# Expert weights dealt to partitions in 16 KB runs, gather and transposes on strided columns

## What is computed

```
n2 = rms_norm(h, norm2_w)
top_v, top_i = top_k(n2 @ w_router + b_router, 4);  gates = softmax(top_v)
for each expert e, for its tokens xb:
    gu   = xb @ w_gu[e] + b_gu[e]            # w_gu   (32, 1024, 2048)
    gate = min(gu[:, :1024], 7);  up = clip(gu[:, 1024:], -7, 7)
    act  = gate * sigmoid(1.702 * gate) * (up + 1)
    y    = act @ w_down[e] + b_down[e]       # w_down (32, 1024, 1024)
    h   += y * gate_of_the_token
```

## Time and profile before

| | |
|---|---|
| time, three runs | 1054.03, 1056.91, 1062.96 us (median 1056.91) |
| span of the profiled execution | 1053.6 us |
| what lies around the span, against the median | 3.3 us |
| PE busy | 1002.0 us (95%) |
| DVE, ACT, POOL busy | 212.1, 147.8, 17.8 us |
| moved by DMA | 417.84 MB, mean 397 GB/s |
| DMA packets | 80940, of which 48688 under 8 KB |

### The profile page before, as it was taken

One profiled execution on the slowest core, in us unless ns is written; L12 is line 12 of the kernel. 1 busy time (PEld: TensorE's weight loads), 2 busy tenths in 40 slices (PEclk: granted clock), 3 DMA queues, 4 the chain that ended last, 5 costly groups with the idle time before them and its releaser, 6 DMA issues.

```text
span 1053.6 us, 12628 instructions
## 1 busy us (share of the span) xinstructions
PE 1002.0 (95%) x5069; PEld 436.9 (41%) x5069; DVE 212.1 (20%) x620; ACT 147.8 (14%) x273; POOL 17.8 (2%) x12
## 2 busy tenths in 40 slices
PE   6989999999999999999999999999999999999997
PEld 4455444444444444433443333334433444434443
DVE  1765311111111111111111111111111111101112
ACT  0332111111110111111111011111110111101111
POOL 0050000000000000000000000000000000000000
PEclk9989999999999999999999999999999999999999
DMA  9995899999999999999999999999999999999994
GB/s 328 276 385 205 304 416 415 416 417 416 419 418 418 417 417 418 418 416 419 419 418 417 417 417 417 418 419 420 418 418 417 409 409 417 417 416 417 418 418 192
DMA packets 80940, 417.84 MB, mean 397 GB/s; under 512 B 8336, under 2 KB 9104, under 8 KB 48688
## 3 DMA queue, kind: packets, MB, share of 16 engines
q1 hardware_dynamic: 75840, 415.91, 97.8%
q10 hardware_dynamic: 5072, 1.51, 0.8%
HBM read 416.35 MB, written 1.05 MB: 396 GB/s over the span
## 4 chain that ended last, share of the span: by engine, by line
PE 54%; SPq 20%; DMA 16%; DVE 5%; ACTq 2%; issue 1%; ACT 1%
PE ps L986 26%; SPq L310 20%; DMA ring<-w_gu_dram 16%; PE ps L1053 13%; PE ps L950 7%; PE ps L964 3%; PE ps L857 2%; DVE PT L763 1%; ACTq L424 1%; ACTq L419 1%; PE ps L1029 1%; ACT PR L462 1%; PE ps L1070 0%; PE ps L837 0%; DVE PR L611 0%
## 5 line engine op out<-in xcount | busy, mean ns | idle before, releaser
L986 PE MATMUL ps<-ring,PT 128*64 128x512 f32 x2008 | 453.7, 595 | 17.1 <-DMA ring<-w_gu_dram 15.5
L986 PEld LDWEIGHTS ps<-ring,PT 128*64 128x64 f32 x2008 | 140.2, 137 | 309.7 <-issue 270.0
L1053 PE MATMUL ps<-ring,PT 128*64 128x512 f32 x1020 | 225.9, 595 | 3.4
L751 DVE TENSOR_SCALAR tT<-ps 128x256 f32<-128x256 f32 x64 | 27.2, 425 | 702.1 <-PE ps L986 702.1
L950 PEld LDWEIGHTS ps<-qk,N 128*128 128x128 f32 x1056 | 120.4, 192 | 21.3 <-issue 21.3
L1053 PEld LDWEIGHTS ps<-ring,PT 128*64 128x64 f32 x1020 | 70.5, 137 | 138.7 <-issue 127.9
L950 PE MATMUL ps<-qk,N 128*128 128x64 f32 x1056 | 124.9, 276 | 0.4 <-DVE qk L724 0.4
L510 ACT ACTIVATE tT<-tT 128x256 f32<-128x256 f32 x64 | 26.7, 418 | 484.4 <-DVE tT L751 484.4
L964 PE MATMUL ps<-PT 64*128 64x512 f32 x256 | 63.6, 615 | 0.8 <-ACT PT L516 0.8
L516 ACT COPY PT<-ps 128x512 f32<-128x512 f32 x32 | 18.8, 587 | 218.7 <-PE ps L1053 218.7
L510 ACT ACT_TABLE_LOAD x32 | 41.1, 1283 | 0.6
(11 more groups left out here) (158 smaller groups left out, 328.2 us busy)
## 6 DMA issues: line engine op xcount, KB each, us to landing
ring<-w_gu_dram SPq DMA_DIRECT2D x121, 2048.0 KB, 25.5
ring<-w_down_dram SPq DMA_DIRECT2D x61, 2048.0 KB, 30.5
ring<-w_gu_dram SPq DMA_DIRECT2D x9, 1024.0 KB, 26.0
ring<-w_down_dram SPq DMA_DIRECT2D x8, 512.0 KB, 21.6
ring<-w_in_dram SPq DMA_DIRECT2D x8, 384.0 KB, 7.3
ring<-w_in_dram SPq DMA_DIRECT2D x2, 1024.0 KB, 13.0
ring<-w_out_dram SPq DMA_DIRECT2D x1, 2048.0 KB, 19.2
ring<-w_out_dram SPq DMA_DIRECT2D x2, 1024.0 KB, 24.1
```

Of the source, the lines that this page charges most:

```text
L751: nc.vector.tensor_scalar(gb[:, b, :], gu[:, b, 0, :], LIMIT, None, ALU.min).then_inc(g_ready, 1)
L986: last = mm(ps[64 * j:64 * j + 64, GU + b, :].rearrange("p (f n) -> p f n", f=2), lhs, halves[j][:, :, 256 * b:256 * b + 256], start=start ...
L1053: last = mm(ps[64 * j:64 * j + 64, DWN, :], aT[:, k, 64 * (c - GU_PIECES):64 * (c - GU_PIECES) + 64], rows[:, 512 * j:512 * j + 512], star ...
```

## The change

The rows of an expert are dealt to the partitions in another way. A `w_gu` piece c now covers the rows 256c to 256c+255, and partition p takes the rows 256c+2p and 256c+2p+1, which lie behind each other in memory: one run of 16 KB. A `w_down` piece takes rows 4p to 4p+3 of its half for partition p: again one run of 16 KB. Bytes, pieces, buffers, and the number and order of the DMAs are as before.

The rows that a partition holds set which columns must stand opposite. In the gather, chunk k of `xe` must hold the columns 256(k//2)+2p+(k%2), so the loaded operand is `N2` in every second column. For the down matmuls, the transposes must take every fourth column of `ab`, over both halves b, so all four wait for both halves of the activation, and their counter `aT_psum` is raised once for an expert and no longer twice.

```diff
-    w_gu_k = w_gu.rearrange("e (k p) n -> p (e k) n", p=P)
-    w_dn_k = w_down.rearrange("e (k p) n -> p (e k) n", p=P)
+    w_gu_k = w_gu.rearrange("e (c p k) n -> p (e c) (k n)", c=GU_PIECES, k=2)
+    w_dn_k = w_down.rearrange("e (j p k) n -> p (e j) (k n)", j=2, k=4)
...
                 if c < GU_PIECES:
-                    chunks, row, src = 2, 2 * c, w_gu_k
+                    chunks, row, src = 2, e * GU_PIECES + c, w_gu_k
                 else:
-                    chunks, row, src = 4, 4 * (c - GU_PIECES), w_dn_k
-                dst = ring[:, slot * PIECE:(slot + 1) * PIECE].rearrange("p (k n) -> p k n", k=chunks)
-                n = min(chunks, stop) - skip
-                sp.dma_start(dst[:, skip:skip + n, :], src[:, bass.ds(e * KC + row + skip, n), :]).then_inc(landed[slot], 16)
+                    chunks, row, src = 4, e * 2 + c - GU_PIECES, w_dn_k
+                wide = PIECE // chunks
+                part = slice(skip * wide, min(chunks, stop) * wide)
+                dst = ring[:, slot * PIECE:(slot + 1) * PIECE].rearrange("p (o n) -> p o n", o=1)
+                sp.dma_start(dst[:, :, part], src[:, bass.ds(row, 1), part]).then_inc(landed[slot], 16)
...
-                dve.wait_ge(aT_psum, 2 * n + 2)
+                dve.wait_ge(aT_psum, n + 1)
...
-                        last = mm(ps[:, GAT, k * SLOTS:(k + 1) * SLOTS], N2[:, t, k * P:(k + 1) * P], S1[:, t, :], start=t == 0, stop=t == T - 1)
+                        rows = N2[:, t, k // 2 * 2 * P:(k // 2 + 1) * 2 * P].rearrange("p (q r) -> p r q", r=2)[:, k % 2, :]
+                        last = mm(ps[:, GAT, k * SLOTS:(k + 1) * SLOTS], rows, S1[:, t, :], start=t == 0, stop=t == T - 1)
...
-                for b in range(2):
-                    pe.wait_ge(act_ready, n * 2 + b + 1)
-                    for c in range(2):
-                        last = nc.tensor.transpose(ps[:, DWN, (2 * b + c) * P:(2 * b + c + 1) * P], ab[:, b, c * P:(c + 1) * P], ident)
-                    last.then_inc(aT_psum, 1)
+                pe.wait_ge(act_ready, n * 2 + 2)
+                for r in range(4):
+                    cols = ab[:, :, :].rearrange("p b (q r) -> p r (b q)", r=4)[:, r, :]
+                    last = nc.tensor.transpose(ps[:, DWN, r * P:(r + 1) * P], cols, ident)
+                last.then_inc(aT_psum, 1)
```

More of the change, by code:

```diff
@@ L304, in load_piece @@
                 if c < GU_PIECES:
-                    chunks, row, src = 2, 2 * c, w_gu_k
+                    chunks, row, src = 2, e * GU_PIECES + c, w_gu_k
                 else:
-                    chunks, row, src = 4, 4 * (c - GU_PIECES), w_dn_k
-                dst = ring[:, slot * PIECE:(slot + 1) * PIECE].rearrange("p (k n) -> p k n", k=chunks)
-                n = min(chunks, stop) - skip
-                sp.dma_start(dst[:, skip:skip + n, :], src[:, bass.ds(e * KC + row + skip, n), :]).then_inc(landed[slot], 16)
+                    chunks, row, src = 4, e * 2 + c - GU_PIECES, w_dn_k
[3 more added lines that the diff above has]
+                sp.dma_start(dst[:, :, part], src[:, bass.ds(row, 1), part]).then_inc(landed[slot], 16)
             def load_ahead(n):
-                src = w_gu_k[:, (NE - 2 * TURN + n // 2) * KC, :].rearrange("p (f j n) -> p j f n", f=2, j=2)
+                src = w_gu_k[:, (NE - 2 * TURN + n // 2) * GU_PIECES, 0:2 * FF].rearrange("p (f j n) -> p j f n", f=2, j=2)
                 sp.dma_start(ahead[n], src[:, n % 2]).then_inc(ld_ahead[n // 2], 16)
@@ L329, in _ @@
             load_piece(6)
-            sp.dma_start(down_ahead, w_dn_k[:, (NE - 2 * TURN) * KC, :]).then_inc(ld_down_ahead, 16)
+            sp.dma_start(down_ahead, w_dn_k[:, (NE - 2 * TURN) * 2, 0:DM]).then_inc(ld_down_ahead, 16)
             sp.wait_ge(PT_psum, 2)
@@ L365, in _ @@
                 if s == 3 * TP - 3:
-                    chunks, row, src, first = 2, KC - 2, w_gu_k, 0
+                    chunks, row, src, first = 2, NE * GU_PIECES - 1, w_gu_k, 0
                 else:
-                    row = 4 * (s - (3 * TP - 2))
-                    chunks, src, first = 4, w_dn_k, 2 + row
+                    half = s - (3 * TP - 2)
+                    chunks, row, src, first = 4, (NE - 1) * 2 + half, w_dn_k, 2 + 4 * half
                 dst = ring[:, s % RING * PIECE:(s % RING + 1) * PIECE].rearrange("p (k n) -> p k n", k=chunks)
+                rows = src[:, row, :].rearrange("p (k n) -> p k n", k=chunks)
                 for k in range(chunks):
-                    sp.dma_start(dst[:, k, :], src[:, (NE - 1) * KC + row + k, :]).then_inc(landed_last[first + k], 16)
+                    sp.dma_start(dst[:, k, :], rows[:, k, :]).then_inc(landed_last[first + k], 16)
             def next_pass(p, r):
```

## The result

The changed kernel takes 1053.37 us (median of 8 runs, 1050.74 to 1056.36), the kernel before 1061.25 us (8 runs, 1054.03 to 1065.26) on the same chip: a ratio of 0.9941, with a 95% interval of 0.9913 to 0.997. That is 7.9 us won where 17 were forecast. The sign is right, the size is not. The profiled execution of the changed kernel has a span of 1050.4 us, against 1053.6 before.

A forecast was written before the change was run, and what follows sets the result against it. PE was taken to bound twenty experts and the DMA twelve, the DMA costing 21.5 us. Span 1053.6 less 16.6 for longer runs, strides and waits at nothing, plus 3.3 around it: 1040 us, range 1034 to 1058.

The forecast's parts named there:

- Longer runs, 16.6 us: Weight loads in the expert loop: 16 KB runs reach 428 GB/s, 0.73 us less an expert, 16.6 us won.
- the rival of 1050 us: Weight loads: runs over 8 KB bring nothing, 29.82 us an expert, 6.8 us won, 1050 us; chance 15%.
- the prediction's 6.6 us: Weight loads: the gain if a packet's fixed cost is the skill page's three beats, 6.6 us instead of 16.6.
- Strided columns at nothing: PE's gather and transpose loads: a step between columns costs nothing; upper bounds 116 us and 0.46 us an expert.
- break-even of 20: Gather's 1056 loads: a slowdown of 20 ns a load, 21 us in all, would eat the gain.
- The clock left out: PE's clock in the expert loop: granted at nine tenths or more throughout, so no term was given to it.
- 3.3 us around the span: Outside the profiled span: 3.3 us added to the span of 1037.0 us, giving 1040.3 us.
- The waits and issues: Transposes' merged wait and SP's DMA issues: 1.3 us of cover, so no cost; fewer runs an issue, worth nothing.
- 8 KB as a ceiling: Weight loads: runs over 8 KB bring nothing, all pieces at 422 GB/s, 29.82 us an expert, 1050 us; chance 15%.
- a gather that doubles: Gather's loads on PE: twice the column time, 116 us more, 1151 us; chance 16% for slower gather loads.
- The transposes did get dearer: Expert loop on PE: only the transposes slow down; doubled they add 14.7 us, 1050 us or 1043; chance 6%.
- a slower DMA: Weight loads: another memory pattern makes the DMA 1% slower, 7 us lost, 1064 us; chance 3%.

The follow-up runs named there:

- r2: Changed kernel with its long runs, but operands stored in the order TensorE reads them, so no load has a step: 1049.08 us, ratio 0.9902 to the kernel before.
- r18: Changed kernel with GpSimd's bias work moved after the softmax and TensorE's gap before the first expert filled: 1045.25 us.
- r16: Kernel of r11 with TensorE's gap before the first expert filled by a repeated product: 1040.88 us, ratio 0.9821 to the kernel before.
- experiment 5: Runs with TensorE's gap before the first expert filled: changed kernel 1052.29 us, control 1052.93; with later bias work too, kernel before 1056.11, changed kernel 1045.25.
- r12: Changed kernel with each piece loaded by two DMAs in runs of 8 KB, in the new memory order: 1050.18 us in one execution.
- r7: Changed kernel with the gather's columns read in a step of four instead of two: 1230.71 us.
- r3: Kernel before with its own memory order and DMAs, but the changed kernel's strided gather and transposes: 1063.12 us, ratio 1.0033.
- r9: Kernel of r2 once more, unedited, as a control: 1048.23 us.
- r10: Kernel of r2 with the seven weight pieces of the front loaded in runs of 4 KB: 1046.91 us.
- r11: Kernel of r2 with GpSimd's bias work made to wait until the softmax is done: 1043.71 us.

## Why the prediction was right in sign and wrong in size

**Longer runs, 16.6 us: right.** 428 GB/s, 29.37 us an expert in r2, and 4.9 us of waits left, as forecast. The fixed cost of 9.0 ns a run holds over three lengths. The Trainium skill's three beats (DMA: Bandwidth & Descriptors, section Why small descriptors are slow), an estimated 3.5 ns, are too few here: they stood for the rival of 1050 us. (At 3.5 ns for 80 runs fewer in each of 22.7 experts the prediction's 6.6 us should read 6.4.)

**Strided columns at nothing: the step that failed.** This is the term "I take nothing, since a column costs 0.86 ns (55 / 64) and the step only changes which four bytes of a partition are read for it". It measured 0.20 us an expert for the gather and 0.07 for the transposes, 8.4 us in 31 periods. 6 ns a load is far under the break-even of 20 that I had worked out, so the verdict kept its sign. But the bound that I gave ran from 0 to 116 us with no row between, and 0 was the wrong end to stand on for 1056 loads that nothing hides. The price isn't fully on top: a slower PE needs its pieces later, and the 4.9 us of waits vanish with it (23 x (29.39 - 28.54) is 19.6 us, less than the 21 that the eight pieces loaded ahead lasted before). Net 3.5 us; r18 less r16, by their medians on two chips and with the front quiet in both, is 4.4 us.

**The clock left out: the larger part of the miss in time, not in gain.** The sum was made against a profiled execution of 1055.4 us, with 0.996 for its mean clock. That is a quarter of the kernel's runs; its median beside the result was 5.9 us higher. The changed kernel's profile had two falls, 5.2 and 1.7 us. "The clock was granted at nine tenths or more throughout the expert loop, and I leave it out" looked at the loop, and the larger fall stands ahead of it.

The kernel before has such falls too, so they count for less in the difference of the two. Of the 8.7 us by which the gain fell short (7.9 for 16.6), the strides hold 4.0. The quiet fronts gave 10.9 us in place of 7.9, so about 3 more go with the clock ahead of the loop and the softmax, and 1.7 are left, as much as the second fall cost in r18's profile. The runs hardly tell these last two from nothing: three sets of the changed kernel won 7.9, 9.9 and 6.3 us.

**"3.3 us around the span": wrong.** Each execution lies 1.8 us above its own span (1052.2 and 1050.4 here); 3.3 mixed the median with the profile of another run.

**The sum again.** Forecast span 1037.0; + 3.5 strides net, + 0.5 of them in the front, + 6.9 clock, + 2.5 front = 1050.4, the span measured. The last three terms were read from this same profile, so that the sum closes is no test of them. Of the 2.5 us, half is the late `norm_w` of experiment 5 and half the attention, where GpSimd's work meets other instructions of DVE in each profile.

**The waits and issues: right.** The transposes' wait kept its cover, and SP's issues fell from 2.1 to 0.33 us; no gain of their own shows, since r2's loop won just what the longer runs account for. **The rivals:** the period of 29.82 us that 8 KB as a ceiling would give came out in r12, whose runs are 8 KB, but not in this kernel; a gather that doubles needs a step of four (r7). The transposes did get dearer, by 15% and not to double. No run speaks for a slower DMA.

## What to carry to other kernels

When two resources are nearly even, removing the waits of one lays bare more of every small cost of the other: of the same 8.4 us of strides 2.2 showed in the loop of r3, where the DMA still bound ten experts, and 3.5 in the changed kernel. Store what TensorE loads in the order in which it is read, if an engine with time to spare writes it (VectorE's two products of an expert took 1.15 us in r2 instead of 0.75, beside idle time); where a step must stay in loads that nothing hides, two floats are cheap and four are not. And before a forecast is added to a profile, ask which of the kernel's runs that profile is: a fall of the clock ahead of the loop may be worth as much as the edit.

## What had not been expected of the hardware

- The rate of full DMA engines depends on the length of a run up to 16 KB: 410, 422 and 428 GB/s.
- Packets of 16 KB (612 ns each at 428 GB/s) delay the short rows of another queue: `w_router` landed after 41 us, and after 30 with 4 KB packets beside it (r9, r10).
- A DVE instruction of 128x4 took 3.92 us beside GpSimd and 0.17 alone (r9, r11).
- PE's clock fell to 1.2 GHz behind a gap of 1.1 to 1.6 us in some profiles and not in others, and in none of four with the gap filled. A second fall, at expert 28 (33.99 us in place of 32.3), comes while PE is busy without a break, and so does one behind the slow gather of r7; what brings them wasn't found.
